# Level masks of a blocked triangular inverse: applied by GpSimd to the matrix, with a plain ScalarE copy after the first product

## What is computed

```python
def step(S, inp):
    r_t, w_t, k_t, v_t, kk_t, a_t = inp
    sa = jnp.einsum('bhvk,bhk->bhv', S, -kk_t)
    S = (S * w_t[:, :, None, :] + sa[..., None] * (kk_t * a_t)[:, :, None, :]
         + v_t[..., None] * k_t[:, :, None, :])
    return S, jnp.einsum('bhvk,bhk->bhv', S, r_t)
```

## Time and profile before

| | us |
|---|---|
| three runs, median (lowest to highest) | 2753.5 (2753.1 to 2755.22) |
| profiled execution, its own time | 2754.43 |
| its span in the trace | 2752.6 |
| busy: PE, DVE, ACT, POOL | 2546.9, 1083.8, 454.8, 1115.3 |
| chunk stage: first pair product of step 0 to first x product of step 8 | 1158.85 to 1380.87 |

### The profile page before, as it was taken

One profiled execution on the slowest core, in us unless ns is written; L12 is line 12 of the kernel. 1 busy time (PEld: TensorE's weight loads), 2 busy tenths in 40 slices (PEclk: granted clock), 3 DMA queues, 4 the chain that ended last, 5 costly groups with the idle time before them and its releaser, 6 DMA issues.

```text
span 2752.6 us, 48984 instructions
## 1 busy us (share of the span) xinstructions
PE 2546.9 (93%) x19851; PEld 2444.2 (89%) x19851; DVE 1083.8 (39%) x1855; ACT 454.8 (17%) x922; POOL 1115.3 (41%) x869
## 2 busy tenths in 40 slices
PE   5999999999999997488868989879999999999998
PEld 4999999999999997278835989868999999999997
DVE  6332133213461444966674521533543213321333
ACT  4110011001120100422243240122211001100102
POOL 3444444444454434531124374003444444444442
PEclk8999999999999998789977999999999999999999
DMA  3111111111132111000022152232111111111111
GB/s 109 46 46 47 49 46 46 46 46 47 41 112 65 43 37 41 0 2 4 4 104 89 34 150 79 81 104 83 55 42 47 49 46 46 46 46 48 48 38 73
DMA packets 220696, 150.24 MB, mean 55 GB/s; under 512 B 10831, under 2 KB 211113, under 8 KB 219946
## 3 DMA queue, kind: packets, MB, share of 16 engines
q1 hardware_dynamic: 217850, 134.91, 16.4%
q10 hardware_dynamic: 2256, 13.71, 1.3%
q0 software_dynamic: 480, 0.05, 0.0%
HBM read 134.60 MB, written 14.04 MB: 54 GB/s over the span
## 4 chain that ended last, share of the span: by engine, by line
PE 88%; DVE 8%; ACT 2%; issue 2%; DMA 0%; POOL 0%; SPq 0%; DVEq 0%; ACTq 0%; POOLq 0%
PE bank L378 25%; PE bank L380 25%; PE bank L379 25%; PE bank L1156 1%; PE bank L1660 1%; PE bank L1629 1%; PE bank L1693 1%; PE bank L1165 1%; PE bank L1141 1%; DVE z L835 1%; DVE Ti L1062 0%; DVE cum L854 0%; DVE y_nat L1852 0%; PE bank L1229 0%; DVE PM L1046 0%
## 5 line engine op out<-in xcount | busy, mean ns | idle before, releaser
L351 POOL TENSOR_TENSOR w_hi<-raw,cst 128x512 fp32r<-128x512 f32 x366 | 464.5, 1269 | 1230.8 <-PE bank L380 1052.8
L378 PE MATMUL bank<-h_hi,w_lo 128*128 128x344 f32 x2856 | 914.5, 320 | 8.9 <-issue 7.5
L380 PE MATMUL bank<-h_hi,w_hi 128*128 128x344 f32 x2856 | 913.1, 320 | 0.0
L379 PE MATMUL bank<-h_lo,w_hi 128*128 128x344 f32 x2856 | 912.4, 319 | 0.0
L378 PEld LDWEIGHTS bank<-h_hi,w_lo 128*128 128x128 f32 x2856 | 535.9, 188 | 10.9 <-issue 9.2
L356 POOL TENSOR_TENSOR w_lo<-raw,w_hi 128x512 fp32r<-128x512 f32 (+1 forms) x398 | 514.3, 1293 | 65.3 <-ACT w_hi L348 35.6
L380 PEld LDWEIGHTS bank<-h_hi,w_hi 128*128 128x128 f32 x2856 | 536.1, 188 | 1.1
L379 PEld LDWEIGHTS bank<-h_lo,w_hi 128*128 128x128 f32 x2856 | 534.8, 187 | 1.4
L380 PE MATMUL bank<-hid_hi,w_hi 128*128 128x344 f32 x1056 | 337.3, 319 | 0.0
L378 PE MATMUL bank<-hid_hi,w_lo 128*128 128x344 f32 x1056 | 337.2, 319 | 0.0
L379 PE MATMUL bank<-hid_lo,w_hi 128*128 128x344 f32 x1056 | 337.1, 319 | 0.0
(11 more groups left out here) (305 smaller groups left out, 2871.3 us busy)
## 6 DMA issues: line engine op xcount, KB each, us to landing
raw<-in_ffn_gate SPq DMA_DIRECT2D x88, 256.0 KB, 2.8
raw<-in_ffn_up SPq DMA_DIRECT2D x88, 256.0 KB, 2.8
raw<-in_ffn_down SPq DMA_DIRECT2D x80, 256.0 KB, 2.7
raw<-in_w_in SPq DMA_DIRECT2D x44, 256.0 KB, 2.8
cache<-in_cache_mem_k SPq DMA_DIRECT2D x8, 1024.0 KB, 5.1
cache<-in_cache_mem_v SPq DMA_DIRECT2D x8, 1024.0 KB, 5.0
x_save<-x ACTq DMA_DIRECT2D x1, 4128.0 KB, 12.5
x<-x_save ACTq DMA_DIRECT2D x8, 516.0 KB, 6.5
```

Source lines behind the costliest of these rows:

```text
L351: nc.gpsimd.tensor_tensor(w_hi[part], raw[part], cst[:, C_ONE:C_ONE + 1, 0:ph["width"]].to_broadcast([P, nk, ph["width"]]), ALU.mult)\
L378: nc.tensor.matmul(out, b, hi, start=first, stop=False)
L379: nc.tensor.matmul(out, a, lo, start=False, stop=False)
L380: m = nc.tensor.matmul(out, a, hi, start=False, stop=last)
```

## The change

GpSimd gets ten new multiplications for each block, two for each level (`level_pool`): it masks `PM` itself for that level into one of two new tiles `Lo` of 128x512. `y_tensor` then multiplies `Lo` and `Ti`, and waits for the tile (`Lo_made`). The product needs no mask any more, and ScalarE copies it to `Ym` (`y_scalar`, ten copies of 128x256 for each block); VectorE's ten masked copies of a block are gone. The masks in the table are those of the matrix, on the other side of the diagonal. The `Lo` of a level waits until the y products of the level two before it have been made.

```diff
-    def low(lv):
-        return (i >> (lv + 1) == j >> (lv + 1)) & (j >> lv < i >> lv)
+    def upper(lv):
+        return (i >> (lv + 1) == j >> (lv + 1)) & (i >> lv < j >> lv)
...
+        Lo = [at(f"Lo{q}", [P, 2, 4, CH], arena_w + 18432 + 2048 * q) for q in (0, 1)]
...
+        def y_scalar(act, m, lv):
+            for hp in (0, 1):
+                k = 10 * m + 2 * (lv - 1) + hp
+                act.wait_ge(S("Y_t"), k + 1)
+                act.wait_ge(S("D_t"), max(k - 1, 0))
+                nc.scalar.activation(Ym[:, hp], y_bank(m, lv, hp)[:, 0:256].rearrange(
+                    "p (h t) -> p h t", h=4), ACT.Copy).then_inc(S("Y_ev"), 1)
...
             if m < 7:
                 scale_scalar_ex(act, m + 1)
+            if m < 8:
+                y_scalar(act, m, 1)
             if n >= 0:
                 u_scalar(act, n, 1)
+            if m < 8:
+                y_scalar(act, m, 2)
+            if n >= 0:
+                out_scalar(act, n, 1)
             if m < 7:
                 scale_scalar_in(act, m + 1)
-            if n >= 0:
-                out_scalar(act, n, 1)
+            for lv in (3, 4, 5) if m < 8 else ():
+                y_scalar(act, m, lv)
...
+        def level_pool(g, m, lv):
+            for hp in (0, 1):
+                g.wait_ge(S("pair_ev"), 4 * m + hp + 1)
+                g.wait_ge(S("Y_t"), max(10 * m + 2 * (lv - 3) + hp + 1, 0))
+                nc.gpsimd.tensor_tensor(Lo[(5 * m + lv) % 2][:, hp], PM[m % 2][:, 0, hp, 0],
+                                        level_mask(lv), ALU.mult).then_inc(S("Lo_made"), 1)
+
         def chunk_pool(g, n):
+            m = n + 1
             if n < 0:
                 scale_pool(g, 0)
-            else:
+            if m < 8:
+                level_pool(g, m, 1)
+                level_pool(g, m, 2)
+            if n >= 0:
                 state_pool(g, n, 0)
+            if m < 8:
+                level_pool(g, m, 3)
+            if n >= 0:
                 state_pool(g, n, 1)
+            if m < 8:
+                level_pool(g, m, 4)
+                level_pool(g, m, 5)
             if n < 6:
                 scale_pool(g, n + 2)
...
-        def y_vector(dve, m, lv, hp):
...
             for lv in range(1, NLV + 1) if m < 8 else ():
-                for hp in (0, 1):
-                    y_vector(dve, m, lv, hp)
...
         def y_tensor(pe, m, lv, hp):
             pe.wait_ge(S("T_flip"), 10 * m + 2 * (lv - 1) + hp + 1)
+            pe.wait_ge(S("Lo_made"), 10 * m + 2 * (lv - 1) + hp + 1)
...
-                             PM[m % 2][half(ck), 0, hp, 0, ht, :], Ti[half(ck), hp, ht, :],
+                             Lo[(5 * m + lv) % 2][half(ck), hp, ht, :], Ti[half(ck), hp, ht, :],
```

More of the change, by code:

```diff
@@ L61, in constants @@
             np.where(first, up0, i == j), s <= t]
-    tabs += [np.where(first, low(lv), low(lv + 1)) for lv in (1, 3, 5)]
+    tabs += [np.where(first, upper(lv), upper(lv + 1)) for lv in (1, 3, 5)]
     return np.stack([np.asarray(m, np.float32) for m in tabs], 1)
@@ L902, in mask, with level_mask @@
             return cst[:, table:table + 1, CH * part:CH * part + CH].to_broadcast([P, n, CH])
-        def low_mask(lv):
+        def level_mask(lv):
             return mask(C_LVL + (lv - 1) // 2, (lv - 1) % 2, 4)
```

## The result

The change makes the kernel slower: 2770.07 us in the median of four runs (2765.03 to 2773.47) against 2753.3 (2751.67 to 2755.22), a ratio of 1.0059 [1.004, 1.0078]. The forecast was 2762.5, the range 2754 to 2772. The profiled execution is the fastest of the four, 2765.03 with a span of 2762.9: 10.3 us more than before.

The account below looks back on a forecast made before the run. Bound: one TensorE-VectorE chain with little slack. Steps 3 to 7 +3.4, steps 0 to 2 +1.3, -3.3, +1.0 and +2.0, low clock +4.7: +9.1 on 2754.4, median 0.9 lower, forecast 2762.5 us, range 2754 to 2772.

Parts of the forecast that it names:

- level 5: Steady steps, end of the levels: ScalarE, idle there, copies `Ym` earlier, so d's second half starts sooner; -0.25 us a step.
- GpSimd's masks: Level 0 of steady steps: masks beside VectorE delay L1057 and `stc`; together +0.46 us a step.
- ScalarE's queue at level 1: Steady steps: the copy to `Ym` stands behind the exponentials, so d of level 1 starts later; +0.52 us a step.
- second `PM` late, by L1057 beside a mask: Level 0, first half of heads: L1057 alternates with a GpSimd mask, delaying the second `PM` and pair product; +0.31 us.
- x, by `stc`: Level 0, second half of heads: VectorE's `stc` comes 0.31 us late, of which 0.15 us is charged to x.
- levels 2 to 4: Steady steps: no cost, since TensorE's other products between y and d still cover the copy; 0 us.
- Steps 0 to 2: First steps: step 0 +1.3 and, at its end, -3.3; step 1 +1.0; step 2 +2.0 us.
- second rival: The clock holds from step 1 on and this pays for the rest: sum -0.1, 2753.5 us; chance 0.15.
- Step 2's term: Step 2: four masks ahead of `std` behind the token shift delay `stc`; +2.0 us, ends +0.6 and +3.7.
- The clock in steps 3 to 7: Steady steps: longer TensorE waits bring two low-clock stretches, +4.7 us; one to four give +2 to +10.
- third rival: Half clock comes at the second pair product in all of steps 3 to 7: 2773 us; chance 0.10.

Follow-up runs that it names:

- e2: GpSimd half alone: masks as in the change, the copy to `Ym` stays on VectorE without a mask; 2774.22 us, ratio 1.0076.
- e6: The change, with level 1 and 2 masks waiting for VectorE's level 0 of their half, and a step's first `std` ahead of them; 2756.22 us, ratio 1.0014.
- e11: e8 with the masks of level 2 waiting for VectorE's L1022 (`ext`); 2739.61 us, ratio 0.9954.
- e5: The change, with ScalarE's two copies of level 1 issued ahead of the three exponentials; 2773.53 us, ratio 1.0065.
- e8: e7 with the last two pieces of the token shift spread behind GpSimd's work of steps 1 to 6; 2741.14 us, ratio 0.9956.
- e7: The change with the edits of both e5 and e6; 2753.6 us, ratio 1.0003.
- e3: The change plus idle TensorE transpositions: 9 ahead of the second pair product, 2 before and 2 after d of level 1; 2764.03 us, ratio 1.0046.
- second profile: The change unchanged, run and profiled again: median 2771.93 us, ratio 1.0069, profile span 2768.7.
- e4: The kernel before, with the long VectorE instruction of steps 0 and 1 issued behind level 5's masked copies; 2752.76 us, ratio 1.0001.
- e10: The kernel before, with the token shift spread and the long instruction of steps 0 and 1 behind level 5's copies; 2741.81 us, ratio 0.9959.

## Why the prediction was right or wrong

**The direction and the mechanisms in a clean step were right; the sizes were not all.** The kernel is slower, by the two costs named, and level 5 gives back what was said. Per clean step, GpSimd's masks were predicted at 0.46 and cost 0.80 (e2 against before; 0.48 of it comes back in e6 and 0.32 in e11), ScalarE's queue at level 1 was predicted at 0.52 and cost 0.40 (e5), and level 5 at -0.25 and gave -0.21 (e11 against before).

| step of the prediction, clean step | predicted | measured |
|---|---|---|
| second `PM` late, by L1057 beside a mask | +0.31 | +0.41 (1.70 - 1.29) |
| x, by `stc` | +0.15 | +0.39 (pair product to x: 4.06 against 3.67) |
| level 1, d behind the exponentials | +0.52 | +0.57 (x to d: 3.19 against 2.62) |
| level 5 | -0.25 | -0.22 |
| level 1, d to the y of level 2 | 0 | -0.17 (1.52 against 1.69) |
| levels 2 to 4 | 0 | 0.00 |
| sum | +0.73 | +0.98 (the step: 0.99) |

*Level 1.* The 0.52 took the start of d, 1287.56, for the whole of d. Before, the first d product ran while the last u products were still running, so its train stretched to 1288.86; in the change d starts behind all of u and runs straight on, and that gives 0.17 back.

*L1057.* The 0.31 rested on alternation with 0.47 us turns, taken from the earlier trace rows. The order was right, the turn was not: L1089 ended as late as 0.83 after its start, 0.41 more than alone: the first mask ended 0.58 after L1088 (1285.16 to 1285.74), not 0.47. In e8 the first mask, beside which VectorE ran no instruction with two inputs in SBUF, took 0.73 us, not the 0.62 of `std`, from which I had taken its turn: 0.11 more, as the turn was.

*`stc`.* The 0.15 left L1022 uncharged; `ext` on L1054 met `std` and took 0.82 instead of 0.67, and with the second L1089's 0.41 `stc` came 0.55 later after the pair product (3.59 against 3.04). My sentence on the Trainium skill's rule (SBUF — State Buffer, section "Who interferes with whom") was right here and my sum without it was not: by that rule L1022 is held as well, and it was, by 0.15 in the change. Where e7 and e8 moved the masks behind the level 0, it was held for 0.49 (1.16 against 0.67), and e11, which keeps them apart, gains 0.32 us a step.

*Steps 0 to 2.* Together +1.0 was predicted; the profiles give -1.0 and +5.2. Step 0: the wait of 1.86 went, d ran straight on, and the pair product came at 1184.80, behind the additions to `TT`, as named. Not foreseen was the half clock at the step's beginning: 0.51 up to 1170.00 against 0.84 before. In the change d of level 1 came 11.28 us after the stage's start (1159.29 to 1170.57), before 8.65, which is 2.6 more where 1.6 was predicted. Step 1 kept full clock in the first profile, which was the second rival's condition, and was 5.9 us shorter. The rival's sum of -0.1 still missed that profile's 10.3 by 10.4: 2.5 in steps 0 to 2, 1.0 in the clean steps, 5.0 in the low stretches of step 3, which it had left out, and 1.9 outside the stage.

**Step 2's term failed**: +2.0, with ends of +0.6 and +3.7, against +4.5 and +8.4. The mechanism was the one named (four masks and the token shift ahead of `std`). What I had wrong is the end of the token shift: I took it as fixed at 1228.37, but the shift moves with step 1, and it ended at 1226.35 in the first profile and 1227.19 in the second. So `stc` did not come 0.6 us later than before but 1.1 and 0.25 earlier. Step 2 had begun 5.0 and 4.2 us earlier, so the wait swallowed most of what step 1 had won, where I let it swallow only the 1.86 us at the end of step 1. The other part is the clock: from `stc` on, the rest of the step took 0.6 us longer than before in the first profile and 4.5 in the second, after 8 us of waiting at the lower level.

*The clock in steps 3 to 7.* Two stretches at +4.7 were forecast; one step with +5.0 in the first profile (in it two stretches, one behind the wait for the second `PM` and a longer one from 1265.6 on), two with +6.7 in the second. The mechanism, a longer wait for the second `PM`, fits the counts above: 9 of 20 steps with 1.70 us of it, 6 of 45 with 1.29, none of 5 in e3. What failed is that I took one profile's picture of before as fixed: "I take two such stretches" has no row that gives their number, and two profiles of the same kernel differ in it. My 9.1 is close to the first profile's 10.3, but against the median the forecast is 7.6 us too low. The second profile, 7.0 above the forecast's sum, divides this: 1.0 in the clean steps (4.4 against 3.4), 4.2 in steps 0 to 2, 2.0 in the low stretches of steps 3 to 7, and -0.2 outside. The third rival's time, 2773, is near the second profile's, but not by its mechanism: in neither profile did all of steps 3 to 7 fall.

Still open: where the low stretches lie in the runs without a profile, and why e3's timed runs lie above its profile. e4's profile, too, at 2749.9 is 2.9 below its median.

## What to carry to other kernels

Work moved to an idle engine costs what it collides with and what stands ahead of it in that engine's queue: look up which instruction of the chain starts at the same event (`PM` here), and let the moved work wait for a later one (e6 and e11 took back 0.48 and 0.32 us of a step's 0.99 so). Compare kernels by the length of a clean step before comparing totals, since the two profiles of the change differ by 5.8 us of span with every clean step alike. A removed wait need not show in the total: in e4's profile steps 0 to 2 are 6.7 us shorter, and its median is level with before; only with the token shift spread as well (e10) did the total fall clearly.

## What the runs showed that was not expected

The same instructions were granted low clocks in different steps in two runs (step 3, then steps 1, 5 and 7). The Trainium skill (TensorE: Matmul & The Clock Gate, Part 1) says that the same kernel can meet the clock's transitions at different points from run to run, and the two profiles of the change agree that it does: 32.10 and 27.13 us for one and the same step 3.

Idle work cost nothing in the total: with 13 transpositions a step, which add 0.13 us to a clean step, the median was 6 to 8 us lower, though the intervals of the ratios overlap. And a removed wait of 1.86 us went with a step 6.0 us shorter in e4's profile, where the clock was 1.00 instead of 0.81.

Part of this clock's time is not tied to the change at all: the profile of before has steps 1 and 2 at 0.81 and 0.78, and two kernels without the change have a low step among 3 to 7, e4 in step 4 (29.20 us) and e10 in step 3 (29.19), both at 0.88. e11 has one as well (28.98 us, 0.88).
